# Two levels of scores to a visit of TensorE in the gated recurrence of a hybrid decoder step

## The reference, cut to what matters

```
proj = h @ w_in; q, f, i, g = split(proj, 4)            # per head: 1024 -> 128, four times
fg = lb + (1 - lb) * sigmoid(f);  log_f = log(fg);  k = (1 - lb) * sigmoid(-f)
# per chunk, b = cumsum(log_f), S the state of the chunk's start:
o_inter = (q * exp(b)) @ S
scores  = sum_k q_t * exp(b_t - b_s) * k_s   for s <= t
o       = o_inter + scores @ v
S_new   = exp(b_end) * S + (k * exp(b_end - b)).T @ v
o = o * rsqrt(mean(o * o) + EPS) * gnorm * silu(g);  out = o @ w_out
```

## Time and profile before

| | us |
|---|---|
| median of 3 runs | 2344.11 (2341.58 to 2347.11) |
| profiled execution, device time | 2343.07 |
| its span in the trace | 2341.3 |
| mean granted TensorE clock | 0.994 of full speed |

### The profile page before, as it was taken

One profiled execution on the slowest core, in us unless ns is written; L12 is line 12 of the kernel. 1 busy time (PEld: TensorE's weight loads), 2 busy tenths in 40 slices (PEclk: granted clock), 3 DMA queues, 4 the chain that ended last, 5 costly groups with the idle time before them and its releaser, 6 DMA issues.

```text
span 2341.3 us, 43951 instructions
## 1 busy us (share of the span) xinstructions
PE 2285.6 (98%) x18176; PEld 2241.9 (96%) x18176; DVE 1206.4 (52%) x1707; ACT 676.2 (29%) x809; POOL 2.8 (0%) x15
## 2 busy tenths in 40 slices
PE   7999999999999999999999999999989999999998
PEld 7999999999998789999999999999988999999998
DVE  4766765456777754332344684233347444323443
ACT  4222222234344332221222322122353332212223
POOL 0000000000000000000000000000000000000000
PEclk9999999999999999999999999999999999999999
DMA  4224443242323034323322322322234432223312
GB/s 132 82 74 117 134 119 99 72 110 68 93 73 84 28 97 113 99 67 102 104 73 86 91 72 76 99 78 82 67 116 160 107 90 72 81 81 90 89 57 74
DMA packets 391480, 211.24 MB, mean 90 GB/s; under 512 B 22657, under 2 KB 385362, under 8 KB 391378
## 3 DMA queue, kind: packets, MB, share of 16 engines
q1 hardware_dynamic: 380114, 198.03, 30.2%
q10 hardware_dynamic: 11264, 11.77, 1.5%
HBM read 193.01 MB, written 20.94 MB: 91 GB/s over the span
## 4 chain that ended last, share of the span: by engine, by line
PE 87%; DVE 9%; issue 2%; ACT 1%; DMA 0%; ACTq 0%; DVEq 0%; SPq 0%
PE ps L1924 81%; PE ps L2115 2%; DVE w_lo L1127 1%; PE ps L1893 1%; DVE o_rs L1665 1%; DVE rstd L1148 1%; PE ps L2278 1%; PE ps L2289 0%; PE ps L2265 0%; DMA w_raw<-in_ffn_w_in_dram 0%; PE ps L2023 0%; PE ps L2181 0%; PE ps L2163 0%; PE ps L2172 0%; DVE t_a L1153 0%
## 5 line engine op out<-in xcount | busy, mean ns | idle before, releaser
L1924 PE MATMUL ps<-h_hi,w_hi 128*128 128x288 f32 x3328 | 725.2, 300 | 12.7 <-DVE t_a L1153 10.1
L1924 PE MATMUL ps<-h_hi,w_lo 128*128 128x288 f32 x3328 | 713.4, 296 | 0.0
L1924 PE MATMUL ps<-h_lo,w_hi 128*128 128x288 f32 x3328 | 713.0, 296 | 0.0
L1924 PEld LDWEIGHTS ps<-h_hi,w_hi 128*128 128x128 f32 x3328 | 535.6, 189 | 26.2 <-DVE t_a L1153 10.3
L1924 PEld LDWEIGHTS ps<-h_lo,w_hi 128*128 128x128 f32 x3328 | 537.1, 189 | 0.0
L1924 PEld LDWEIGHTS ps<-h_hi,w_lo 128*128 128x128 f32 x3328 | 537.0, 189 | 0.0
L1127 DVE TENSOR_TENSOR w_lo<-w_raw,w_hi 128x2048 fp32r<-128x2048 f32 (+3 forms) x184 | 369.9, 2010 | 153.8 <-ACT w_hi L691 151.8
L691 ACT ACTIVATE w_hi<-w_raw 128x2048 fp32r<-128x2048 f32 (+3 forms) x184 | 309.6, 1683 | 256.6 <-PE ps L1924 242.8
L1924 PE MATMUL ps<-g_hi,w_hi 128*128 128x288 f32 x1408 | 302.4, 296 | 0.0
L1924 PE MATMUL ps<-g_hi,w_lo 128*128 128x288 f32 x1408 | 301.6, 295 | 0.0
L1924 PE MATMUL ps<-g_lo,w_hi 128*128 128x288 f32 x1408 | 301.5, 295 | 0.0
(11 more groups left out here) (346 smaller groups left out, 1697.7 us busy)
## 6 DMA issues: line engine op xcount, KB each, us to landing
w_raw<-in_ffn_w_in_dram SPq DMA_DIRECT2D x176, 512.0 KB, 4.9
w_raw<-in_ffn_w_out_dram SPq DMA_DIRECT2D x64, 384.0 KB, 4.2
w_raw<-in_ffn_w_out_dram SPq DMA_DIRECT2D x64, 320.0 KB, 3.6
w_raw<-in_hgrn_w_in_dram SPq DMA_DIRECT2D x32, 512.0 KB, 5.3
w_raw<-in_s_w_glu_dram SPq DMA_DIRECT2D x16, 512.0 KB, 5.0
wc_d<-c_pow ACTq DMA_DIRECT2D x8, 512.0 KB, 3.4
wb_d<-wb_st ACTq DMA_DIRECT2D x8, 512.0 KB, 3.6
s_in<-in_state_hgrn_dram SPq DMA_DIRECT2D x8, 512.0 KB, 4.8
```

The lines of the kernel that those rows point to most:

```text
L1924: ins = M.matmul(ps[:, 2 * s + h, 0:HALF], w[j][:, at:at + P], v[:, k, h * HALF:(h + 1) * HALF], start=k == 0 and n == 0, stop=k == ph.kt ...
```

## The change

Two more buffers, `q_x` and `k_x`, are added. Where q and k of each level lie is now given by `q_at` and `k_at`, so that the inputs of two neighbouring levels exist at the same time. TensorE works two levels in a visit. VectorE updates q and k twice and then selects twice. Where an update goes from one buffer to the other, it writes only the half that it multiplies, and ScalarE copies the other half (`hold`, for levels 2, 4 and 6). The update of level 0 is made at the end of the step before. The visits of a step are now seven, at new cuts; `sums` and `v_turned` are both in the third. VectorE's `chain` now comes before the last quarter of the reciprocal and before `normalise`. The parts of the closing step are dealt out anew (`CLOSING`).

```diff
+        def q_at(b, n):
+            return q_x if n in (1, 2, 5, 6) else q_t[b]
+        def k_at(b, n):
+            return k_x if n in (3, 4, 7, 8) else k_t[b]
...  (ScalarE)
+                def hold(m, b, n):
+                    act.wait_ge(qk_done, m * LEVELS + n)
+                    nc.scalar.activation(level_halves(q_at(b, n + 1), n)[:, :, 0], level_halves(q_at(b, n), n)[:, :, 0],
+                                         ACT.Copy)
+                    nc.scalar.activation(level_halves(k_at(b, n + 1), n)[:, :, 1], level_halves(k_at(b, n), n)[:, :, 1],
+                                         ACT.Copy).then_inc(held_done, 1)
...
                     elif m is not None:
                         split(PH[n_ph + 1], 1, 0, ph, None)
+                    if m is not None:
+                        hold(m, 1 - b, 2)
+                        hold(m, 1 - b, 4)
                     if n is not None and not last:
                         project_f(n, b)
...
                         take_turned(m, vt_full, v_tok, vtok_done)
+                        hold(m, 1 - b, 6)
...  (VectorE)
+                def levels(m, b, p):
+                    update(m, b, 2 * p + 1)
+                    if p < LEVELS // 2 - 1:
+                        update(m, b, 2 * p + 2)
+                    select(m, 2 * p)
+                    select(m, 2 * p + 1)
...
                     invert(before, 2)
+                    if m is not None:
+                        chain(m, mb, turn)
                     invert(before, 3)
                     normalise(before)
-                    if m is not None:
-                        chain(m, mb, turn)
                     o_rest(before)
...  (TensorE)
+                def levels(m, b, p):
+                    if p == 0 and (not isinstance(m, int) or m):
+                        pe.wait_ge(on_done, m)
+                        pe.wait_ge(s_out_done, m)
+                    pe.wait_ge(qk_done, m * LEVELS + (2 * p + 1))
+                    if p:
+                        pe.wait_ge(held_done, m * 3 + p)
+                        pe.wait_ge(sc_read, m * LEVELS + 2 * p)
+                    level(b, 2 * p)
+                    level(b, 2 * p + 1)
...
+                CLOSING = {2: ((0, 0, 5),), 3: ((0, 5, 6), (1, 0, 3)), 4: ((1, 3, 4),), 5: ((1, 4, 5),), 6: ()}
...
-                    cuts = (3, 6, 9, 13, 16, 19, 22, 25, 28, 30, 32)
-                    if n is not None and last:
-                        cuts = (2, 4, 6, 9, 11, 13, 16, 18, 20, 22, 24)
+                    cuts = (2, 7, 12, 17, 19, 21, 24) if last else (3, 9, 16, 22, 25, 28, 32)
...
                         if m is not None:
-                            if at < LEVELS:
-                                level(m, 1 - b, at)
-                            if at == SAMPLE_LEVELS and (not isinstance(m, int) or m):
-                                pe.wait_ge(sc_read, m * LEVELS + SAMPLE_LEVELS)
-                                sums(m)
-                            if at == SAMPLE_LEVELS + 1:
+                            if at < LEVELS // 2:
+                                levels(m, 1 - b, at)
+                            if at == 2:
+                                if not isinstance(m, int) or m:
+                                    pe.wait_ge(sc_read, m * LEVELS + SAMPLE_LEVELS)
+                                    sums(m)
                                 v_turned(m)
-                            if at == LEVELS:
-                                k_turned(m, 1 - b)
-                            if at == LEVELS + 1:
+                            if at == 4:
+                                k_turned(m)
+                            if at == 5:
                                 chunk_adds(m)
                                 sampled_adds(m)
...
                 step(None, 0, HEADS - 1)
-                out_part(1, 3, 4)
                 sums(HEADS)
-                out_part(1, 4, HEADS - 2)
+                out_part(1, 5, HEADS - 2)
```

More of the change, by code:

```diff
@@ L456, in back_bank, with level_halves @@
             return {NK - 2: 4, NK - 1: 6}.get(ct, 2)
+        def q_at(b, n):
+            return q_x if n in (1, 2, 5, 6) else q_t[b]
+        def k_at(b, n):
+            return k_x if n in (3, 4, 7, 8) else k_t[b]
+        def level_halves(ap, n):
+            half = HALVINGS[n - 1]
+            span = T if half < DEC_SEQ else SEQ
+            return ap[:, 0:span].rearrange("p (n h l) -> p n h l", h=2, l=half)
         def turned_back(ct):
@@ L1576, in hgrn @@
                 reciprocal(1)
-                for t in (k_pad[0], k_pad[1], v_pad):
+                for t in (kx_pad, v_pad):
                     V.memset(t[:, T:T_PAD], 0.0)
                 link(V.memset(score[:], 0.0))
-                def level(m, b, n):
-                    dve.wait_ge(sc_full, m * LEVELS + (n + 1))
[L1585 to L1605, removed]
@@ new lines, in update @@
+                def update(m, b, n):
+                    if n == 0:
+                        dve.wait_ge(gates_done, m + 1)
+                        dve.wait_ge(free[0], m * 2 + (ph.tile0 + 1))
+                        V.tensor_tensor(q_at(b, 1)[:], q_at(b, 0)[:], f_t[:], ALU.mult).then_inc(qk_done, 1)
+                        return
+                    if n == 3 and (not isinstance(m, int) or m):
+                        dve.wait_ge(decay_done, m)
+                    half = HALVINGS[n - 1]
+                    span = T if half < DEC_SEQ else SEQ
+                    blocks = span // (2 * half)
+                    at = {1: None, 2: 0, 4: 288, 8: 432, 16: 504, 32: 536, 64: 552, 128: 560}
+                    e = f_t[:, 0:span] if half == 1 else e_t[:, at[half]:at[half] + span // half]
+                    e = e.rearrange("p (n h) -> p n h", h=2)
+                    out = e_t[:, at[2 * half]:at[2 * half] + blocks]
+                    shape = [P, blocks, half]
+                    if n % 2:
+                        dve.wait_ge(sc_full, m * LEVELS + (n + 1))
+                    dve.wait_ge(qk_done, m * LEVELS + n)
+                    V.tensor_tensor(level_halves(q_at(b, n + 1), n)[:, :, 1], level_halves(q_at(b, n), n)[:, :, 1],
+                                    e[:, :, 0:1].to_broadcast(shape), ALU.mult)
+                    V.tensor_tensor(level_halves(k_at(b, n + 1), n)[:, :, 0], level_halves(k_at(b, n), n)[:, :, 0],
+                                    e[:, :, 1:2].to_broadcast(shape), ALU.mult)
+                    V.tensor_tensor(out, e[:, :, 0], e[:, :, 1], ALU.mult).then_inc(qk_done, 1)
@@ L1700, in step @@
                         take(pre[:], 1, n, 0)
-                    if m is not None and not last:
-                        level(m, mb, 4)
-                        if n is None:
-                            rest(PH[n_ph + 1], 1, 0)
-                        level(m, mb, 5)
-                    invert(before, 0)
+                    if m is not None:
+                        levels(m, mb, 2)
+                    if last:
+                        dve.wait_ge(silu_g, n)
+                        take(pre[:], 1, n, 0)
+                    if n is None and m is not None:
+                        rest(PH[n_ph + 1], 1, 0)
                     if n is not None and not last:
                         gates(n, b)
+                    invert(before, 0)
                     if m is not None:
-                        level(m, mb, 6)
+                        levels(m, mb, 3)
                     if n is not None and not last:
@@ L1714, in step @@
                         take(v_t[:], 0, n, 1)
-                    if m is not None:
-                        level(m, mb, 7)
-                    if n is not None and not last:
                         invert(before, 1)
@@ L1735, in step @@
                         take(pre[:], 1, n, 1)
+                    if n is not None:
+                        update(n, b, 0)
                     if m is not None:
@@ L2098, in hgrn, with level @@
             def hgrn(ph):
[L2099 to L2109 removed]
+                def level(b, n):
+                    q, k = q_at(b, n), k_at(b, n)
                     last, side = n == LEVELS - 1, P // 2
```

52 lines of the change are left out of this document (23 added, 29 removed).

## The result

| | before | after |
|---|---|---|
| median of 20 runs, us | 2343.57 (2339.98 to 2347.11) | 2348.30 (2343.80 to 2352.60) |
| ratio to before | | 1.0020, 95% interval 1.0013 to 1.0027 |
| profiled execution: device time, span, us | 2343.07, 2341.3 | 2343.80, 2342.1 |

The changed kernel is slower by 0.2%, 4.7 us in the medians. The forecast was 2349.3 us and +5.2. The profiled execution of the changed kernel is the fastest of its 20, so its trace shows the steps and the waits but not the whole distance of the medians.

What follows compares the result with a forecast made beforehand. TensorE, busy 98% of the span, was taken as the bound. Loop steps +3.6, head 1 -1.1, head 7 -3.8 and closing step +4.3 make +3.0; clock falls +2.2 give +5.2, 2349.3 us, range 2339 to 2357.

Steps and rivals of the forecast that it cites:

- The wait before `v_turned`: Third visit of five loop steps: TensorE stands 2.2 us until ScalarE's root, behind the sigmoids, is done; bounds 0.5 to 2.6.
- A merged visit: TensorE's visits go from 11 to 7 a step, each crossing saving 0.28 us, together 1.1 us a step.
- The loop step: Steps of heads 2 to 6: -1.1 crossings, -0.4 chain wait, +2.2 stall, so +0.7 us each and +3.6 for five.
- Head 1's step: Step without `sums` or root: only the crossings are saved, -1.1 us.
- Head 7's step: Waits fall from about 5.1 to 4.0, crossings save 1.1 and the clock 1.6: -3.8 us, bounds -6 to -1.
- The closing step: Waits +3.8, two more k-steps before `tail` +1.6, four crossings less -1.1: +4.3 us, bounds +2 to +6.
- this order ends before `tail` does and costs nothing: VectorE's list after the chain moves ahead: `o_rest`, waiting about 0.8 us for `o_high`, and level 0's update are covered.
- The clock: Gaps of about two microseconds on TensorE can lower the clock, about 1.5 us each; one or two falls, +2.2 us.
- the copies or selections become the bound: Rival: the second visit waits in each step, +1 us times 7, 2356 us; chance 0.07.
- the clock falls nowhere: Rival: the new gaps stay harmless, +3.0 us, 2347.1 us; chance 0.27.
- at every gap: Rival: the clock falls at all seven gaps, 1.5 us each, 2357.6 us; chance 0.13.
- the root did hold `v_turned`: Opposite rival: the root is done in time, the loop step shrinks by 1.5 us, -9.3 in all, 2334.8 us; chance 0.13.

Runs made afterwards that it cites:

- e3_root_first: Changed kernel with ScalarE's root ahead of the two sigmoids in all steps but the closing one; 2340.19 us, ratio 0.9984 to before.
- e9_root_sums_first: Changed kernel with the root ahead of the sigmoids (not in the closing step) and `sums` ahead of levels 4 and 5; 2335.04 us, ratio 0.9963 to before.
- e4_gap: Changed kernel with a k-step between the two levels of the first, second and fourth visit in seven steps; 2359.57 us, ratio 1.0067 to before.
- e5_chain_alone: Kernel before with only VectorE's `chain` moved ahead of the last quarter of the reciprocal and `normalise`; 2340.61 us, ratio 0.9990 to before.
- e6_rest_alone: Kernel before with only the low part of a weight moved behind levels 2 and 3 in head 7's step; 2339.57 us, ratio 0.9989 to before.
- e0_after: The changed kernel run once more, unedited, beside other experiments on one chip; 2347.17 us, ratio 1.0017 to before.
- e2_hold_first: Changed kernel with ScalarE copying the halves for level 2 ahead of the output weights' split in the closing step; 2345.79 us, ratio 1.0010 to before.
- e7_part_behind: Changed kernel with one k-step of the output projection moved from the closing step to behind `tail`; 2348.51 us, ratio 1.0030 to before.

## Why the prediction was right

The time, the sign and the main mechanism came out as forecast: 2348.3 for 2349.3, +4.7 for +5.2. Step by step:

- **The wait before `v_turned`.** Priced at 2.2, measured 2.10, in exactly the five loop steps; in head 7's and the closing step 0.92 where I had 1.2. e3_root_first shows the cause: the root ahead of the sigmoids takes away 1.18 of it, and with `sums` ahead of the levels too (e9_root_sums_first) the rest goes.
- **A merged visit.** Priced at 0.28 a crossing. e4_gap gives 0.37. The loop step itself says the same: 40.19 - 0.58 (the chain, from e5) + 2.10 - 40.54 = 1.17 for four, 0.29 each, or 0.34 with the chain at the 0.39 of its row. The two differ because the first matmul of `tail` starts 0.27 behind a product but 0.43 where there was a wait, the wait itself taken off (e5_chain_alone).
- **The loop step** came out at +0.35 where I had +0.7; the wait was 0.1 smaller, and the chain and the crossings gave 0.2 and 0.1 more than their rows said. Five steps are +1.8 in place of +3.6 (five times +0.7 is 3.5; the prediction's figure is 0.1 too high).
- **Head 1's step**: -1.1 forecast, -1.35 measured.
- **Head 7's step**: -3.8 forecast, -3.9 measured, with the waits at the places given and near the sizes (1.23, 0.92 and 1.47 for 1.2, 1.2 and 1.6). e6_rest_alone shows that moving the low part of the weight alone gives 3.7; the crossings and the chain then about pay for the new waits. The figure holds where the clock does not fall; in e0_after it did, and the step gained 2.3.
- **The closing step**: +4.3 forecast, 33.62 - 29.54 = +4.1 in e0_after. Its parts were not all right. The wait of 2.0 was 1.88, and e2_hold_first shows its cause. But one of the two k-steps that I priced at 0.8 each costs nothing by e7_part_behind: its place is covered by the late copy of k. (The other was not tried.) What I left out is behind the step, +0.6. VectorE adds to the sampled state of head 7 behind `o_rest`. In the kernel before that was at 818.89, 2.6 us ahead of the squares. Now TensorE gets to `tail` with the last quarter of the reciprocal, `normalise` and `o_rest` still to come on VectorE, the addition starts level with the squares, and `sums` waits 1.46 for it:

```profile
824.51 1.22 DVE L1693 TENSOR_TENSOR s_out<-s_out,ps 128x1024 f32<-128x1024 f32 x1
```

The prediction says that this order ends before `tail` does and costs nothing. That holds in the loop, not in the closing step.

- **The clock.** One or two falls at 1.5 forecast. The four traces with the loop's stall of 2.1 and its step unmoved (after, e0, e2, e7) have 1, 1, 2 and 1 falls in their five loop steps, 0, 1, 0 and 0 in head 7's and 1, 0, 0 and 1 in the closing step: two falls in each of the four. A loop step with a fall is 41.94 to 42.06, so the price is 1.4 to 1.5. e4_gap, which has the same five stalls, shows three falls in the loop and one in head 7's step. The one of head 7's step in e0 is not at a gap of two microseconds, where alone I had looked for them.

Without falls the sum of the steps is -1.35 + 1.8 - 3.9 + 4.1 + 0.6 = +1.3 where I had +3.0; with the two falls of each trace it is about +4.2, and the traces of after and e0_after sum to +4.3 and +3.9. The medians say +4.7 and, on e0's chip, +3.1. So the structural sum was 1.7 too high, mostly the loop step's term, and the falls were taken 0.7 too low. The two errors partly cancel, and that the total came out within 1 us is partly luck. What stays open is the last microsecond: how often the clock falls over many runs can't be read from medians, and the stretch after the closing step ran at the lower clock for 3.4 to 13.7 us in different traces with the same code.

Of the rivals, the case that the copies or selections become the bound is excluded: no loop step of the changed kernel has a wait at its second or fourth visit. That the clock falls nowhere, or at every gap, is excluded by the traces too, and the root did hold `v_turned`. The Trainium skill's drain of 1380 ns behind a table load (ScalarE: Activation LUTs, What ACT_TABLE_LOAD costs) doesn't appear after the change either: the load at 607.62 takes 1.28 and the root starts at 608.91.

## What to carry to other kernels

Putting two small jobs into one visit of the busy engine saves a crossing each, but takes away the work that stood between a result and its next use; before merging, list what each job hands to another engine and how long the answer takes, here 4.3 us against 2.0 of work. A stall of that kind is cured by order, not by distance: the answer ahead of what does not need to be first (root before sigmoids), and independent work between question and use (levels between `sums` and `v_turned`). Moving the use itself later can be worse, since its own successors are then late. And what stands behind the work that is put in between becomes later too: in the closing step of e9_root_sums_first that cost 1.0 us.

## What the runs showed of the hardware

After TensorE had stood still for 2.10 us in a loop step, the granted clock went from 2.4 to 1.2 GHz in 8 of 25 cases (after, e0_after, e2_hold_first, e7_part_behind, e4_gap), though the steps are alike in every row. Each such stretch at the lower clock lasted 3.4 us and made the step 1.4 to 1.6 us longer. The gap of 1.88 us in the closing step was followed by one in 2 of 7 traces. A gap of 3.20 us in head 7's step was followed by one in each of the two traces that have it (before, e5_chain_alone).

The length of the last gap alone does not decide it. Five gaps of 0.92 us in loop steps (e3_root_first) were followed by no fall, but one of 0.90 us in e4_gap was, and one of 1.47 us in e0_after was, where the same gap of 1.47 us in the trace of the changed kernel was not.
